# Expert rows gathered in quarter rows through one buffer and turned by VectorE, with the activation transposes amid the next block's gate products

## The chip, the cores and the metric

The kernel runs on one core of one Trainium2 chip. A core has TensorE (matrix products and transposes, written to eight PSUM banks), VectorE, ScalarE, GpSimd (POOL in the profile) and SyncE (SP), which here issues DMAs. Sixteen DMA engines move data for all of them; SP's DMAs stand in one queue of the profile (q1), POOL's in another (q0). The metric is the device time of one execution in microseconds, the median of several runs.

## The reference, cut to what matters

One inference step of a hybrid decoder layer for 1024 prompt tokens and 64 sample tokens (1088 rows of 1024 floats, all float32). Three residual sublayers stand one after the other: attention and a convolution, cross attention to a memory, and a mixture of experts. The change concerns the last:

```python
x = x + hier_moe(rmsnorm(x, norm_ffn_g), w_rg, b_rg, w_re, b_re, w_gate, w_up, w_down)

def hier_moe(h, w_rg, b_rg, w_re, b_re, w_gate, w_up, w_down):
    lg = t @ w_rg + b_rg                       # 4 groups, the best is taken
    le = (t @ w_re + b_re).reshape(-1, 4, 8)   # its 8 experts, the best 2 are taken
    ...
    act = jax.nn.silu(t @ w_gate[e]) * (t @ w_up[e]) * comb[:, e]
    y = sum over the chosen e of act @ w_down[e]
```

There are 32 experts, each with gate and up weights of 1024x256 and down weights of 256x1024, 1 MB apiece. A token goes to two experts.

## The kernel before

**Stages.** Up to about 600 us of the span come the mixer and the sample group's part; then the prompt's cross attention tile by tile (nine tiles of tokens, tile 0 is the 64 sample tokens), with the router of each tile in it. In that stage VectorE writes Z3, the tile's rows after the norm and without the gain, which are stored to a scratch tensor in DRAM, z3 (`z_scratch` in the profile). Z3 is written with its columns permuted (`by_row`), so that column k * 128 + p holds feature 8p + k, the order in which the experts' weights are loaded. TensorE turns Z3 for the router, and VectorE multiplies by the gain vector (`V_FFN` in `cvec`) as it takes the result out of PSUM (line 2318). A sort on VectorE and TensorE then makes the lists: `TABLE`, `PERM` and `PSEL` are multiplied on TensorE (`place`) into the indices of the tokens of each block.

**Blocks.** The experts are computed in 24 blocks (`NB`) of 128 rows, each divided into four parts of 32 rows (`PART`); a part belongs to one expert, and a block has one, two or more experts (`COLUMNS`, in the order `BLOCKS`). `tiles_of(n)` gives each part its weight slot. Seven slots hold the weights of seven experts; the other 25 experts are loaded by SP during the blocks, gate and up as soon as the gate products of the last block that uses a slot are done (`gu_done`), down as soon as its down products are (`dn_done`). A row list has unfilled places; their index lies out of bounds and the DMA drops the row. Rows beyond the lists' room would go through a loop at the end, which has no instruction in this trace.

**A block's path.** POOL gathers its 128 rows of 4 KB from z3 into `ZG` (one buffer, an indirect DMA, line 760). TensorE turns them, eight transposes of 128x128 into banks 0 and 1 (`turn_rows`, line 1388, semaphore `zt4_done`). VectorE takes them out with the gain into `HG[n % 2]` (`take_rows`, line 2430, `hg_ready`). TensorE computes gate and up (`gate_up`, line 1401, 64 instructions, four parts side by side), ScalarE the silu (1793), VectorE the product with up and the token's gate (`activate`, line 2434, `ab_ready`). TensorE turns that with two transposes (line 1431, `at_done`), ScalarE copies them out (1795, `at_ready`), TensorE computes down (`down`, line 1408, 32 instructions), ScalarE and VectorE take the halves out (1800, 2450), and POOL adds the rows to the outputs with two indirect DMAs (766 for the prompt's, 768 for the sample's; rows of the other output are dropped).

**Order.** It is written out by hand. TensorE's step n is: gate and up of block n + 1, activation transposes of block n, row transposes of block n + 2, down of block n. VectorE's step n: activation of n, rows of n + 2, second half of n's result. POOL's loop issues the gather of block n + 1 when block n has been turned, then the adds of block n - 3. SP's loop issues weights as slots come free. Every semaphore is waited for by the engine's own program, in that order.

Of the kernel before, what the change touches and what calls it, by code (L numbers as in the profile page):

```python
# [38 lines left out]
def rank_of(g, j):  # L39
# [16 lines left out]
assert BLOCKS[0] == 0 and [c[2:4] for c in COLUMNS[0]] == [(0, 2), (0, 2)]  # L56
QUARTER = [[k for k, b in enumerate(COLUMNS) if len(b) == 2 and b[1][2:4] == (q, 1)] for q in range(5)]
NSEL = len(FIRST) + len(SECOND)
CONSTS = [("ident", 128), ("mean", 128), ("dist", 256), ("dist_s", 772), ("tri", 128), ("sel", NSEL + 2), ("caps", NE), ("ones", 128),
          ("iota", POS), ("tri33", 33), ("tok", NT), ("thr", 8), ("o16", OVER)]  # L60
# [8 lines left out]
def shape_constants():  # L69
# [23 lines left out]
    put("iota", np.tile(np.arange(POS)[None, :], (128, 1)))  # L93
    put("tri33", (np.arange(32)[:, None] < np.arange(33)[None, :]) * 1.0)
# [44 lines left out]
def build(nc, i, o):  # L139
# [7 lines left out]
    with ctx:  # L147
# [26 lines left out]
        rid_i = sb("rid_i", NE, i32)  # L174
        cap_e = sb("cap_e", 1)
# [88 lines left out]
        tri, sel, caps, ones, iota, tri33, tok, thr, o16 = (rc(n) for n in ("tri", "sel", "caps", "ones", "iota", "tri33", "tok", "thr", "o16"))  # L264
# [39 lines left out]
        HG = [view(W, ROUT + 2048 + 1024 * r, DC, 128) for r in range(2)]  # L304
        YB = [view(W, ROUT + 4096 + 1024 * r, D) for r in range(2)] + [view(W, ROUT + 1024, D)]
        EB = [view(W, ROUT + 6144 + 256 * r, FE) for r in range(2)]
# [51 lines left out]
        for name, (first, count) in {  # L358
# [30 lines left out]
            "over_t": ("zt4_done", 2 * NB),  # L389
            "over_h": ("hg_ready", 2 * NB),  # L390
# [89 lines left out]

        def spread_pt(mt, b):
# [22 lines left out]
        def _(sp):  # L504
# [18 lines left out]
            sp.dma_start(cvec[:, V_FFN:V_FFN + DC], i["norm_ffn_g"][0].rearrange("(p c) -> p c", c=DC)).then_inc(M["small_in"], 16)  # L523
# [9 lines left out]
            sp.dma_start(wr[:, :, 0:NG], i["w_router_group"][0].rearrange("(p c) n -> p c n", c=DC)).then_inc(M["wr_in"], 16)  # L533
            sp.dma_start(wr[:, :, NG:36], i["w_router_expert"][0].rearrange("(p c) n -> p c n", c=DC)).then_inc(M["wr_in"], 16)
# [88 lines left out]
            for it in range(NT + 2):  # L623
# [13 lines left out]
                if s2 == 0:  # L637
# [12 lines left out]
                    load_mo(4, DC)  # L650
                if s2 == NT - 1:
# [55 lines left out]
        def _(pool):  # L707
# [55 lines left out]

            def add_rows(at_p, at_s, buf, landed):
# [1738 lines left out]
```

## Time and profile before

| | us |
|---|---|
| median of 3 runs | 1276.28 (1275.07 to 1276.29) |
| the profiled execution | 1268.7 |
| its span, first to last instruction | 1266.9 |
| TensorE busy | 1168.5 (92%) |
| VectorE busy | 675.2 (53%) |
| ScalarE busy | 323.1 (26%) |
| POOL busy | 146.8 (12%) |
| mean granted TensorE clock | 0.968 |

Times in the rows are microseconds from the start of the span unless marked ns. "idle before" is what the engine stood still ahead of an instruction, with what ended it. PE is TensorE, PEld its loading of the stationary operand, which runs beside the products; DVE is VectorE, ACT ScalarE. A transpose is a matrix product with the identity and stands in the profile as MATMUL. A float32 product stands as two instructions, a transpose as one. The DMA share is the mean busy share of the sixteen DMA engines; since the packets' times overlap a little it can pass 1.

### The profile page before, as it was taken

The numbers are of one execution on the slowest core, as the hardware profiler recorded it, in microseconds if no ns is written. First come the engines' busy times: TensorE is split into PE (matmuls) and PEld (weight loads), VectorE is DVE, ScalarE is ACT, GpSimd is POOL, SyncE is SP. The second block draws the span as 40 slices with busy tenths as digits, with TensorE's granted clock in tenths as the row PEclk, the third lists the DMA queues.
The fourth block names the chain that finished last, engine by engine and source line by source line (L and its number), as shares of the span: only waits on it lengthen the run. The fifth ranks groups of instructions, "written<-read, shape, count | busy, mean of one in ns | idle before, by whom it ended". The sixth has DMA issues, their size and how long they took to land.

```text
span 1266.9 us, 17480 instructions
## 1 busy us (share of the span) xinstructions
PE 1168.5 (92%) x6415; PEld 594.5 (47%) x6415; DVE 675.2 (53%) x2085; ACT 323.1 (26%) x934; POOL 146.8 (12%) x159
## 2 busy tenths in 40 slices
PE   6988879999999999998999999999787999999995
PEld 3434536545555555553555565556442333333331
DVE  1118689999999999831345454545554222222220
ACT  1124434443453456421111111111110101110110
POOL 0000000000000000300000000000001223333332
PEclk9997899999999999999999999999897999999997
DMA  8871000030000002357110011000587998999992
GB/s 317 306 252 46 1 1 26 17 150 34 1 34 34 1 26 114 151 205 312 33 51 23 28 50 50 34 1 34 207 355 311 397 336 319 364 378 385 387 332 53
DMA packets 48914, 194.89 MB, mean 154 GB/s; under 512 B 12240, under 2 KB 15094, under 8 KB 36515
## 3 DMA queue, kind: packets, MB, share of 16 engines
q1 hardware_dynamic: 37883, 173.79, 35.3%
q0 software_dynamic: 10368, 17.87, 5.8%
q10 hardware_dynamic: 576, 2.10, 0.4%
q8 instruction: 52, 0.85, 0.3%
q14 instruction: 35, 0.29, 0.1%
HBM read 172.60 MB, written 42.36 MB: 170 GB/s over the span
## 4 chain that ended last, share of the span: by engine, by line
PE 50%; DVE 4%; DMA 2%; issue 1%; ACT 0%; POOL 0%; SPq 0%; POOLq 0%; DVEq 0%
PE bank L1401 13%; PE bank L843 9%; PE bank L1347 9%; PE bank L1408 7%; PE bank L1325 3%; PE bank L1285 2%; PE bank L1388 2%; PE bank L1126 1%; DMA W<-in_w_mo 1%; DMA W<-in_cache_mem_k 1%; PE bank L1204 1%; DVE G L1848 1%; PE bank L1431 1%; DMA W<-z_scratch,idx_i 1%; PE bank L849 1%
## 5 line engine op out<-in xcount | busy, mean ns | idle before, releaser
L843 PE MATMUL bank<-W,G 128*128 128x512 f32 (+1 forms) x768 | 314.6, 565 | 3.8 <-DVE G L1848 3.0
L1904 DVE SCALAR_TENSOR_TENSOR W<-W,dwT 128x128 f32<-128x128 f32 (+1 forms) x1048 | 271.8, 335 | 0.0
L843 PEld LDWEIGHTS bank<-W,G 128*128 128x128 f32 x768 | 145.4, 192 | 151.0 <-issue 147.6
L1401 PE MATMUL bank<-W 128*32 128x512 f32 x1152 | 155.8, 595 | 1.0 <-DVE W L2430 0.9
L1347 PE MATMUL bank<-W 128*128 128x512 f32 x256 | 115.2, 599 | 0.2 <-DVE W L2309 0.2
L715 POOL TENSOR_SCALAR st<-st 128x1 f32<-128x1 f32 (+3 forms) x40 | 13.7, 343 | 874.7 <-DVE st L2005 434.1
L1126 PE MATMUL bank<-W 128*128 128x512 f32 x256 | 111.8, 594 | 0.0
L2430 DVE TENSOR_TENSOR W<-bank,cvec 128x512 f32<-128x512 f32 x48 | 31.0, 686 | 145.7 <-PE bank L1388 145.7
L1401 PEld LDWEIGHTS bank<-W 128*32 128x32 f32 x1152 | 43.7, 110 | 82.5 <-issue 80.9
L1408 PE MATMUL bank<-W 128*32 128x512 f32 x576 | 81.7, 602 | 0.5 <-ACT W L1795 0.5
L1126 PEld LDWEIGHTS bank<-W 128*128 128x128 f32 x256 | 47.9, 190 | 57.4 <-issue 56.9
L1347 PEld LDWEIGHTS bank<-W 128*128 128x128 f32 x256 | 46.7, 190 | 51.6 <-issue 51.5
L1401 PE MATMUL bank<-G,W 128*32 128x512 f32 x384 | 63.4, 592 | 1.5 <-issue 1.5
L2450 DVE COPY W<-bank 128x512 f32<-128x512 f32 x24 | 16.6, 691 | 81.9 <-PE bank L1408 81.9
L1795 ACT ACTIVATE W<-bank 128x256 f32<-128x256 f32 x24 | 9.2, 383 | 188.2 <-PE bank L1431 188.2
L1841 DVE TENSOR_SCALAR G<-G,st 128x1024 f32<-128x1024 f32 (+1 forms) x20 | 15.0, 752 | 62.7 <-POOL st L719 53.7
L760 POOL DMA_INDIRECT W<-z_scratch,idx_i x24 | 25.5, 1064 | 182.7 <-PE bank L1388 165.8
L1602 ACT ACTIVATE W<-W,st 128x256 f32<-128x256 f32 (+2 forms) x68 | 32.5, 479 | 39.2 <-DVE st L1969 39.2
L766 POOL DMA_INDIRECT out_y_p<-W,idx_i x24 | 37.8, 1576 | 28.0 <-issue 10.7
L768 POOL DMA_INDIRECT out_y_s<-W,samp_i x24 | 37.3, 1554 | 7.3 <-issue 7.3
L1408 PEld LDWEIGHTS bank<-W 128*32 128x32 f32 x576 | 20.2, 110 | 33.9 <-issue 33.2
L1325 PE MATMUL bank<-W,G 128*128 128x128 f32 x256 | 31.8, 284 | 4.2 <-DVE W L2303 4.2
(324 smaller groups left out, 1467.3 us busy)
## 6 DMA issues: line engine op xcount, KB each, us to landing
W<-in_w_exp_gate SPq DMA_DIRECT2D x23, 1024.0 KB
W<-in_w_exp_up SPq DMA_DIRECT2D x23, 1024.0 KB
W<-in_w_exp_down SPq DMA_DIRECT2D x23, 1024.0 KB
G<-in_w_exp_gate SPq DMA_DIRECT2D x9, 1024.0 KB
G<-in_w_exp_up SPq DMA_DIRECT2D x9, 1024.0 KB
G<-in_w_exp_down SPq DMA_DIRECT2D x9, 1024.0 KB
W<-in_cache_mem_k SPq DMA_DIRECT2D x8, 1024.0 KB, 5.0
W<-in_cache_mem_v SPq DMA_DIRECT2D x8, 1024.0 KB, 7.8
```

What stands on the lines that cost most here:

```text
L760: pool.indirect_dma_start(out=buf, out_offset=None, in_=z3_d, in_offset=bass.IndirectOffsetOnAxis(ap=col, axis=0), bounds_check=NTOK - 1, ...
L766: pool.indirect_dma_start(out=yp_flat, out_offset=bass.IndirectOffsetOnAxis(ap=at_p, axis=0), in_=buf, in_offset=None, bounds_check=SEQ - ...
L768: pool.indirect_dma_start(out=ys_flat, out_offset=bass.IndirectOffsetOnAxis(ap=at_s, axis=0), in_=buf, in_offset=None, bounds_check=NS - 1 ...
L843: mm = pe.matmul(bank[0:rows, at:at + hi - lo], HT[:, c, 0:rows], w[:, c, lo:hi], start=(c == 0), stop=(c == DC - 1))
L1126: mm = pe.matmul(B[half][0:n3, :], lhs, w_out[:, c, 512 * half:512 * half + 512], start=(c == 0), stop=(c == 7))
L1325: mm = pe.matmul(B[6 + c // 4][:, (c % 4) * 128:(c % 4) * 128 + 128], MV[:, mt, c * 128:(c + 1) * 128], PT2[:, mt, c // 2, :], start=(mt = ...
L1347: mm = pe.matmul(B[2 + half][0:n2, :], OT2[:, c, 0:n2], w_mo[:, c, 512 * half:512 * half + 512], start=(c == 0), stop=(c == DC - 1))
L1401: mm = pe.matmul(B[2 + par][lo:hi, :], HG[par][:, c, lo:hi], WGU[u][:, :, c, :], start=(c == 0), stop=(c == DC - 1), skip_group_check=True)
L1408: mm = pe.matmul(B[6 + half][lo:hi, :], AT[par][:, c, lo:hi], WD[u][:, c, 512 * half:512 * half + 512], start=(c == 0), stop=(c == 1), ski ...
L1602: act.activation(sh, sh, ACT.Exp, bias=st[:, 50 + h:51 + h], scale=SCALE, accum_out=st[:, 58 + h:59 + h]).then_inc(M["s_exp"], 2 if s2 == ...
L1904: dve.scalar_tensor_tensor(y, src, w, y, ALU.mult, ALU.add).then_inc(M["conv_tap"], 1)
L2430: dve.tensor_tensor(buf[:, 4 * half:4 * half + 4, :], B[half][:, :].rearrange("p (c t) -> p c t", c=4), gain(V_FFN + 4 * half, 4), ALU.mul ...
```

## The change

- **Rows in quarters.** From block 2 (`TURNED`) on, a block's rows come by four indirect DMAs instead of one. Quarter q is 256 columns of `ZG`. On partition 32 s + r it holds segment s (256 floats, 1 KB) of the row r of part q, so each DMA gathers 128 pieces of 1 KB; the indices are 4 * token + s. They are made by 28 small products on TensorE (`place_segments`) and one instruction on VectorE (`seg_i`).
- **Turned by VectorE.** VectorE waits until the four have landed and turns each quarter with one transpose instruction in blocks of 32x32 (`turn_segments`), straight into `HG`, whose layout becomes four parts of 8 x 32. `turn_rows` on TensorE remains for blocks 0 and 1, with a strided read.
- **One buffer.** `ZG` stays the only buffer. The gather of block n + 3 is issued when VectorE has turned block n + 2 (`hg_ready`), and POOL's adds of block n - 1 follow it.
- **Activation transposes.** For blocks 4 to 22 they stand after the first half of the next block's gate products (`within`), otherwise where they were.
- **Gain.** Z3 is written in plain column order and already multiplied by the gain, which comes as a broadcast tile `GB` (loaded by SP behind the w_mo loads, into room that the sample group's scores have left). The router's and the blocks' PSUM reads become plain copies. The router's weights are laid out to match.

```diff
+        def quarters_of(n):
+            return [(q0 + k) * NE + rank_of(g, j) for g, j, q0, count in COLUMNS[BLOCKS[n]] for k in range(count)]
...
+        def rows_landed(n):
+            return 16 * n + 16 if n < TURNED else 16 * TURNED + 64 * (n + 1 - TURNED)
...
+        def rows_turned(n):
+            return 2 * n + 2 if n < TURNED else n + 1 + TURNED
...
+                    sp.wait_ge(M["mkb_used"], DEC_B)
+                    sp.dma_start(GB, i["norm_ffn_g"].to_broadcast([128, D])).then_inc(M["gb_in"], 16)
...
+                if u == 4:
+                    sp.wait_ge(M["z3_ready"], AFTER["z3_ready"] + NT)
                 load_down(sp, expert_id(NEED[u]), u)
...
+            def gather_quarters(n):
+                for q, col in enumerate(quarters_of(n)):
+                    pool.indirect_dma_start(out=ZG[:, 256 * q:256 * q + 256], out_offset=None, in_=z3_segments,
+                                            in_offset=bass.IndirectOffsetOnAxis(ap=seg_i[:, col:col + 1], axis=0),
+                                            bounds_check=4 * NTOK - 1, oob_is_err=False).then_inc(zg_in, 16)
...
-            for n in range(NB + 3):
-                if n + 1 < NB:
-                    pool.wait_ge(M["zt4_done"], 2 * n + 2)
-                    at = BLOCKS[n + 1]
-                    gather(idx_i[:, at:at + 1], zg_in, ZG)
-                if n == 3:
+            gather(idx_i[:, BLOCKS[1]:BLOCKS[1] + 1], zg_in, ZG)
+            pool.wait_ge(M["zt4_done"], 2 * TURNED)
+            pool.wait_ge(M["route_ready"], 3)
+            gather_quarters(TURNED)
+            for n in range(NB + 1):
+                if n + 3 < NB:
+                    pool.wait_ge(M["hg_ready"], rows_turned(n + 2))
+                    gather_quarters(n + 3)
+                if n == 1:
...
-                if n >= 3:
-                    add_block(n - 3)
+                if n >= 1:
+                    add_block(n - 1)
...
+            def place_segments():
+                for q in range(QMAX):
+                    for s in range(4):
+                        mm = pe.matmul(B[7][PART * s:PART * s + PART, NE * q:NE * q + NE], TABLE[0:2 * NE, PART * q:PART * q + PART], PERM[0:2 * NE, :], start=True, stop=True, skip_group_check=True)
+                mm.then_inc(M["r_cols"], 1)
...
+                    if c == DC // 2 and within >= 0:
+                        turn_activation(within)
                     for lo, hi, u in tiles:
-                        mm = pe.matmul(B[2 + par][lo:hi, :], HG[par][:, c, lo:hi], WGU[u][:, :, c, :], start=(c == 0), stop=(c == DC - 1), skip_group_check=True)
+                        mm = pe.matmul(B[2 + par][lo:hi, :], HG[par][:, lo // PART, c, :], WGU[u][:, :, c, :], start=(c == 0), stop=(c == DC - 1), skip_group_check=True)
...
-                    gate_up(tiles_of(n + 1), 1 - p).then_inc(M["gu_done"], 1)
-                pe.wait_ge(M["ab_ready"], n + 1)
...
-                if n + 2 < NB:
-
-                    for mm in turn_rows(n + 3):
-                        mm.then_inc(M["zt4_done"], 1)
+                    gate_up(tiles_of(n + 1), 1 - p, 0, n if n > 3 else -1).then_inc(M["gu_done"], 1)
+                if n <= 3 or n + 1 == NB:
+                    turn_activation(n)
...
-                    dve.tensor_scalar(by_row(Z3[0:n3, :], DC), XB(s3)[0:n3, :].rearrange("p (f c) -> p f c", c=DC), st[0:n3, 41:42], None, ALU.mult).then_inc(M["z3_ready"], 1)
+                    if s3 == 0:
+                        dve.wait_ge(M["gb_in"], AFTER["gb_in"] + 16)
+                    dve.scalar_tensor_tensor(Z3[0:n3, :], XB(s3)[0:n3, :], st[0:n3, 41:42], GB[0:n3, :], ALU.mult, ALU.mult).then_inc(M["z3_ready"], 1)
...
-                        dve.tensor_tensor(H3[:, 4 * half:4 * half + 4, 0:n3], src, gain(V_FFN + 4 * half, 4, n3), ALU.mult).then_inc(M["h3_ready"], 1)
+                        dve.tensor_copy(H3[:, 4 * half:4 * half + 4, 0:n3], src).then_inc(M["h3_ready"], 1)
...
+            def turn_segments(n):
+                dve.wait_ge(zg_in, rows_landed(n))
+                for q in range(4):
+                    a = dve.transpose(HG[n % 2][:, q], ZG[:, 256 * q:256 * q + 256].rearrange("p (f c) -> p c f", c=DC))
+                a.then_inc(M["hg_ready"], 1)
...
                 if n + 2 < NB:
-                    take_rows(None, HG[p], M["zt4_done"], n * 2 + 5, M["hg_ready"])
+                    turn_segments(n + 2)
```

## Rows read from the trace of the kernel before

**Rows 1.** The page's 40 equal slices of the span, TensorE and DMA, in tenths.

```profile
PE   6988879999999999998999999999787999999995
...
DMA  8871000030000002357110011000587998999992
```

**Rows 2.** The critical chain, 1112 to 1142: start, length, engine and line.

```profile
1124.44 0.87 PE bank L1388 x8
...
1136.12 0.87 PE bank L1388 x8
```

**Rows 3.** The timeline of one block and of the last: start, length, engine, line.

```profile
1117.02 7.05 PE L1401 MATMUL bank<-W 128*32 128x512 f32 x64
...
1124.28 1.04 PE L1388 MATMUL bank<-cst,W 128*128 128x128 f32 x8
...
1125.24 3.64 PE L1408 MATMUL bank<-W 128*32 128x512 f32 x32
...
1126.13 1.07 POOL L760 DMA_INDIRECT W<-z_scratch,idx_i  x1 [6.87 <-PE bank L1388]
...
1235.53 0.62 PE L1401 MATMUL bank<-G,W 128*32 128x512 f32 x2 [1.53 <-issue]
```

**Rows 4.** Windows of 20 us: busy time and instructions by engine, clock, DMA share.

```profile
1040.00:1060.00 20.00, 20.00 (x188) 7.22 (x184) 4.88 (x8) 2.51 (x6) 7.54 (x6) 1.00 0.79 266
...
1100.00:1120.00 20.00, 20.00 (x184) 7.14 (x180) 5.16 (x8) 2.51 (x6) 8.40 (x6) 1.00 1.03 374
```

**Rows 5.** SP's issues: down weights (ns, min/median/max), and the last up weight.

```profile
L475 SPq DMA_DIRECT2D W<-in_w_exp_down x23: 337/338/4907, 904.2 to 1204.1; - x23
...
1199.72 3.60 SPq L471 DMA_DIRECT2D G<-in_w_exp_up  x1
```

**Rows 6.** Two lines of VectorE, ns min/median/max: contiguous 256, and strided 1024.

```profile
L2144 DVE TENSOR_SCALAR W<-W,LG x9: 346/353/354, 671.0 to 953.4; 128x256 f32<-128x256 f32 x8, 64x256 f32<-64x256 f32 x1
...
L2267 DVE TENSOR_SCALAR W<-G,st x9: 1294/1337/1354, 611.3 to 941.2; 128x1024 f32<-128x1024 f32 x8, 64x1024 f32<-64x1024 f32 x1
```

**Rows 7.** The critical chain at the stage's first blocks.

```profile
974.23 0.70 issue
974.94 8.53 DMA W<-z_scratch,idx_i
...
988.17 6.87 PE bank L1401 x64
```

**Rows 8.** POOL's lines, 965 to the end: busy us, mean ns, idle before.

```profile
L768 POOL DMA_INDIRECT out_y_s<-W,samp_i x24 | 37.3, 1554 | 7.3 <-issue 7.3
L760 POOL DMA_INDIRECT W<-z_scratch,idx_i x23 | 24.3, 1055 | 165.8 <-PE bank L1388 165.8
```

**Rows 9.** DMA queues in windows 1080:1220, 1138:1141.5, 1142:1145, 1127:1129: packets, MB, share.

```profile
q1 hardware_dynamic: 6020, 43.85, 75.9%
...
q0 software_dynamic: 137, 0.03, 6.8%
...
q1 hardware_dynamic: 108, 0.79, 62.5%
q0 software_dynamic: 108, 0.44, 35.9%
...
q1 hardware_dynamic: 106, 0.78, 92.4%
q0 software_dynamic: 99, 0.03, 8.8%
```

**Rows 10.** The timeline at the start of the stage.

```profile
958.17 1.27 POOL L760 DMA_INDIRECT W<-z_scratch,idx_i  x1 [16.96 <-DVE idx_i L2222]
...
959.18 0.27 PE L1376 MATMUL bank<-W 128*32 128x1 f32 x2 [2.34 <-DVE W L2152]
...
963.35 1.94 PE L1388 MATMUL bank<-cst,W 128*128 128x128 f32 x8 [0.43 <-DMA W<-z_scratch,idx_i]
```

**Rows 11.** Windows around a fall of the granted clock (third number from the right).

```profile
595.00:598.20 3.20, 0.66 (x4) 0.42 (x4) 1.48 (x3) 1.87 (x4) 0.00 (x0) 1.00 0.97 389
598.20:601.60 3.40, 2.74 (x8) 0.89 (x10) 1.02 (x2) 0.53 (x2) 1.95 (x4) 0.50 0.03 6
```

More of the change, by code:

```diff
@@ L56 @@
 assert BLOCKS[0] == 0 and [c[2:4] for c in COLUMNS[0]] == [(0, 2), (0, 2)]
+QMAX = max(max(c) for c in CAPS)
+TURNED = 2
 QUARTER = [[k for k, b in enumerate(COLUMNS) if len(b) == 2 and b[1][2:4] == (q, 1)] for q in range(5)]
@@ L263, in rc @@
             return RC[:, lo:lo + CAT[name][1] - CAT[name][0]]
[L264 removed]
+        tri, sel, caps, ones, iota, seg, tri33, tok, thr, o16 = (rc(n) for n in ("tri", "sel", "caps", "ones", "iota", "seg", "tri33", "tok", "thr", "o16"))
         LG3 = view(LG, 0, NT, 36)
@@ L303, in build @@
         ZG = view(W, ROUT, D)
-        HG = [view(W, ROUT + 2048 + 1024 * r, DC, 128) for r in range(2)]
+        HG = [view(W, ROUT + 2048 + 1024 * r, 4, DC, 32) for r in range(2)]
         YB = [view(W, ROUT + 4096 + 1024 * r, D) for r in range(2)] + [view(W, ROUT + 1024, D)]
+        GB = view(W, 12288, D)
         EB = [view(W, ROUT + 6144 + 256 * r, FE) for r in range(2)]
@@ L1382, in turn_rows @@
             def turn_rows(count):
-                pe.wait_ge(zg_in, 16 * count)
+                pe.wait_ge(zg_in, count)
+                rows = ZG.rearrange("p (f c) -> p c f", c=DC)
                 for half in range(2):
@@ L1387, in turn_rows @@
                         k = 4 * half + c
-                        mm = pe.transpose(B[half][:, c * 128:(c + 1) * 128], ZG[:, k * 128:(k + 1) * 128], ident)
+                        mm = pe.transpose(B[half][:, c * 128:(c + 1) * 128], rows[:, k, :], ident)
                     yield mm
@@ L1394, in tiles_of, with turn_activation, gate_up @@
                 return [(PART * k, PART * k + PART, u) for k, u in enumerate(slots)]
-            def gate_up(tiles, par, upper=0):
+            def turn_activation(n):
+                p = n % 2
+                pe.wait_ge(M["ab_ready"], n + 1)
+                if n == 3:
+                    pe.wait_ge(M["r_taken"], AFTER["r_taken"] + 1)
+                for c in range(2):
+                    mm = pe.transpose(B[4 + p][:, c * 128:(c + 1) * 128], AB[p][:, c * 128:(c + 1) * 128], ident)
+                mm.then_inc(M["at_done"], 1)
+            def gate_up(tiles, par, upper=0, within=-1):
                 for c in range(DC):
@@ L1449, in _ @@
             pe.wait_ge(M["route_ready"], 2)
-            for mm in turn_rows(1):
+            for mm in turn_rows(16):
                 mm.then_inc(M["zt4_done"], 1)
@@ L1454, in _ @@
             gate_up(tiles_of(0), 0, 2).then_inc(M["gu_done"], 1)
-            for mm in turn_rows(2):
+            for mm in turn_rows(32):
                 mm.then_inc(M["zt4_done"], 1)
@@ L1469, in _ @@
                 with pe.Fori(1, OVER + 1) as n:
-                    for mm in turn_rows(n + NB):
+                    for mm in turn_rows(n * 16 + ROWS0):
                         mm.then_inc(M["over_t"], 1)
@@ L1473, in _ @@
                     pe.wait_ge(wgu_in[0], n * 32 + 32 * LOADS[0])
-                    gate_up([(0, 128, 0)], 0).then_inc(M["over_gu"], 1)
+                    gate_up([(PART * k, PART * k + PART, 0) for k in range(4)], 0).then_inc(M["over_gu"], 1)
                     pe.wait_ge(M["ab_ready"], n + NB)
@@ L2424, in over_list, with take_rows @@
                 dve.tensor_copy(gate_s[:, NR:NSLOT], got[:, 1, :]).then_inc(M["over_listed"], 1)
-            def take_rows(banks, buf, done, count, ready):
+            def take_rows(buf, done, count, ready):
                 for half in range(2):
                     dve.wait_ge(done, count + half)
-                    dve.tensor_tensor(buf[:, 4 * half:4 * half + 4, :], B[half][:, :].rearrange("p (c t) -> p c t", c=4), gain(V_FFN + 4 * half, 4), ALU.mult).then_inc(ready, 1)
+                    dve.tensor_copy(buf[:, :, 4 * half:4 * half + 4, :], B[half][:, :].rearrange("p (c q t) -> p q c t", c=4, q=4)).then_inc(ready, 1)
+            def turn_segments(n):
[3 more added lines that the diff above has]
+                a.then_inc(M["hg_ready"], 1)
             def activate(p, e, a, gate):
```

42 lines of the change are left out of this document (23 added, 19 removed).

## The prediction

> **What bounds the kernel now.** I read the page's slices first. In the eight before the last, the expert stage, TensorE stands at 9 in all and the DMA engines at 9 in seven [rows 1]. Two resources are full at once, so the stage has to be read for both.
>
> Then the critical chain: from block 2 to block 22 it is TensorE over and over, gate and up products (L1401), two transposes of the activation (L1431), eight of the next rows (L1388), down products (L1408), with a period of 11.68 us (1124.44 to 1136.12) and no wait [rows 2]. The timeline of one block splits it [rows 3]: gate and up products start at 1117.02, the row transposes at 1124.28, the down products at 1125.24, the next block's gate products 11.68 after the first. The row transposes take 1125.24 - 1124.28 = 0.96 us.
>
> The windows say how full the DMA engines are: 1.03 at 1100 to 1120 and much the same in the windows around it, with one real hole, 0.79 at 1040 to 1060 [rows 4]. The SP queue says it again: a down weight takes 0.338 us to issue in the median but up to 4.9, and the last up weight 3.6, at 1199.72: its queue is full [rows 5]. At the end TensorE stands still for 1.53 us (1234.0 to 1235.53) before the last gate and up products [rows 3], and the row names no engine that it waited for; the weights of the last block were queued on SP only at 1199.72 [rows 5]. So the stage is bound by TensorE by a hair, and TensorE's lead over the weights is used up by its end.
>
> **TensorE, removed.** 22 blocks lose 0.96 us each, 21.1 us. The two activation transposes go into the middle of the next gate products from block 4 on; their time stays, and the array is drained and filled once more there: the products' last start lies at most 0.5 us before the transposes now, I take +0.1. ScalarE's copy then lies under the second half of the gate products, where before it lay under the row transposes: costs nothing. TensorE alone would need 10.8 us a block.
>
> **VectorE.** It loses two PSUM reads a block and gets four transposes of 128x256 each. The trace has none. Nearest rows: 128x256 from SBUF 0.353 us, and a 128x1024 with a strided side 1.33 us, or 0.33 for each 256 [rows 6]. Below: four at 0.3, 1.2 us; above: four at twice the row, 2.8. I take the row itself, 4 x 0.35 = 1.4 us. VectorE is busy 5 of 20 us in the stage [rows 4], so as work it is nothing; but it now stands in a loop.
>
> **The loop through the one buffer.** Before, a gather was issued when TensorE had turned the rows ahead of it, at 1126.13, and had 9.8 us until the transposes 11.68 after 1124.28 wanted it [rows 3]. Now the gather of n+3 is issued when VectorE has turned n+2, and VectorE turns n+3 when all four quarters have landed. These steps follow each other and set a period of their own:
>
> - VectorE done to POOL's first issue: 0.75 (the chain has 0.70 before the issue at 974.94 [rows 7]).
> - Four issues instead of one, each 1.06 [rows 8] with the 0.30 between that the adds show (7.3 us / 24): 1.38 apart, the last starts 4.1 after the first. With two adds of 1.55 and 0.30 POOL needs 9.2 us a block; it fits.
> - Issue to first row: 4.0 us. The gather issued 11.68 us after that of 1126.13, at 1137.81 [rows 3], has moved nothing by 1141.5: POOL's queue shows 137 packets but 0.03 MB in 1138 to 1141.5 (those are the dropped rows of the adds); then in 1142 to 1145 it moves 0.44 MB [rows 9].
> - How the two queues share the engines: 108 packets against 108 in 1142 to 1145, when rows of 4 KB meet weight packets of 8 KB; 99 against 106 in 1127 to 1129, when POOL's packets are nearly all under 512 B [rows 9]. One for one, whatever their size. A weight packet of 8 KB costs 0.759 x 16 x 140 us / 43.85 MB x 8192 B = 0.318 us of one engine [rows 9]. So a gather of 128 rows is 8 packets an engine and waits for 8 weight packets. Check: 4.0 + 8 x (0.16 + 0.318) = 7.8, measured 8.53 to landing [rows 7]: 0.7 for completion.
> - In quarters the gather is 512 packets, 32 an engine. Their own time is small, 1.0 us together (a 4 KB row at half of the 8 KB packet, 0.16; a quarter of that for a quarter row; less for dropped rows). The weight packets between them are not: between 0 and 32 x 0.318 = 10.2 us.
>
> How many meet? 25 experts are loaded in the stage, 24 packets an engine each, over 22 blocks: 27 a block. POOL's queue has 32 + 16 (adds) = 48 a block to pair with them. If the 27 spread evenly over the 48, the gather meets 18: 5.7 us. The period is then 0.75 + 4.0 + (1.0 + 5.7) + 0.7 + 0.1 + 1.4 = **13.65 us**. Once no weights load (the last three intervals) the fourth issue sets it: 0.75 + 4.1 + 4.0 + 0.3 + 0.7 + 0.1 + 1.4 = **11.35**. Ends: none meet, 11.35; all 27, 16.5.
>
> DMA time is no tighter bound. Before, with the holes of [rows 4], it filled nearly all of 11.68; the smaller packets add some 0.2: 11.9 us a block, under 13.65.
>
> The Trainium skill ("DMA: Bandwidth & Descriptors", Queues, rings and completion order) says an engine alternates between queues by packets of several descriptors, typically 9 to 17. By that four or more quarter rows would go for one weight packet, and this loop would not bind (the second rival). The rows on single 4 KB and 8 B pieces speak against it here.
>
> **Start of the stage.** 28 small products (56 instructions) for the quarter lists come on TensorE ahead of that line (L1376). It stands idle for 2.34 us before 959.18 [rows 10]. Four run side by side, as the expert products do (64 in 7.05 us, 16 groups of 0.43 of 512 columns [rows 3]); with 32 columns 0.18 a group is ample: 14 x 0.18 = 2.5 us, so little shows, +0.5. If each of the 56 took 0.12 as one of the eight transposes does (0.96 / 8), 6.7 us, of which 3.5 would show.
>
> **Edits at nothing.** The gain vector's multiplication moves from the router's PSUM reads, which stay as copies of the same size, into the write of Z3 (1.33 us [rows 6], same size, no stride now); nine times a tenth either way. Its 0.5 MB broadcast is queued on SP behind the w_mo loads, for which the output products before the first Z3 wait anyway; were it late, the first tile would wait its 0.5 MB, 1 to 2 us. SP's two new waits, for the score products and for the last Z3, ask for what its next DMA comes after in any case: the sample group's memory values are freed later than its scores are made, and Z3 of the last tile is stored ahead of slot 4's down weights. POOL's adds keep their place, one block's behind one gather.
>
> **Sum, against the profiled execution** (span 1266.9, time 1268.7; the median of the three runs, 1276.28, is 7.6 above it). The chain has block 2's gate products at 988.2, block 23's start at 1235.5 [rows 3, 7]. After: the quarters of block 2 are issued at 974.94 with four weight loads just queued, so all 32 meet: 974.94 + 4.0 + 11.2 + 0.7 + 0.1 + 1.4 = 992.3. Then 18 intervals of 13.65 and 3 of 11.35: 992.3 + 245.7 + 34.1 = 1272.1, +0.5 = 1272.6. That is 37.1 later than 1235.5; the tail of 31.4 us stays. 1276.3 + 37.1 = **1313 us**.
>
> **Rivals.**
> - *Packets of four quarter rows.* Four pieces of 1 KB go at one turn, as the one row of 4 KB did. The gather meets 8 weight packets, 2.5 us, and the period falls to 11.35, under the DMA engines' 11.9. Block 2 starts at 986.1, 2 us sooner, since TensorE no longer waits for rows ahead of the down products; 986.1 + 18 x 11.9 + 3 x 11.35 = 1234.4: **1276**, no change, for the removed transposes only run into the weights. For it: the full DMA share and SP's queue. Against: one for one in both windows.
> - *Faster* (the other side). The same, and the first row comes 2 us after the issue, not 4: the very first gather, of 4 KB rows, took only from 958.17 to TensorE's start on it at 963.35 [rows 10]. The loop is 9.4, TensorE's 10.8 decides until the weights do, and the holes in DMA time (4 us in that of [rows 4]) are filled: **1271**. It decides from the point where the loop is under 11.7. 21 us are not to be had, the weights forbid it.
> - *The clock.* TensorE now stands still for 13.65 - 10.8 = 2.9 us a block. The granted clock was 0.50, the 1.2 GHz level, for 598.2 to 601.6, right after 3.2 us in which TensorE was busy for 0.66 [rows 11]. One such dip of 3.4 us costs 1.7 us: 12.5, still under 13.65. If it stayed at 1.2 GHz (groups of twice 0.43, 24 of them, 21 us a block) it would be 1276 + 21 x 7.7 + 31 = **1470**.
>
> **How the numbers follow.** Main case 0.64; packets of four 0.22; faster 0.10; clock 0.04. The range takes the main case with a turn of 2.8 us (21 x 1.4 = 29 more, 1343) above, and nearly all of "no change" below, 1273; left out are the faster case, the clock, and gathers that meet all 27. 0.2%, 2.5 us, is about what a measurement of this kernel tells from no change. Faster: 0.10 and 0.04 of the second case; same: 0.09 of it; slower: the rest.
>
> **What would show it.** Right: gaps on TensorE before the gate products that end with VectorE's transposes, those waiting for z_scratch DMAs; blocks of uneven length, about 11.4 without and 14 to 18 with weight loads; DMA share under 1; SP's issues back at 0.34 us. Wrong: a period under 12 us, quarters landing under 9 us after the first issue while weights load, or packet counts of POOL's queue well above the weights' in such a window.

## The result: slower, by a third to a little over half of what was forecast

| | kernel before | changed kernel |
|---|---|---|
| runs of this comparison, us | 1275.67 median (1271.91 to 1276.29) | 1288.80 median (1286.47 to 1290.92) |
| ratio | | 1.0118, 95% interval 1.0096 to 1.014 |
| profiled execution, time / span, us | 1268.70 / 1266.9 | 1289.27 / 1287.5 |
| mean granted clock | 0.968 | 0.964 |

The forecast was 1313 us, 37.1 more than before; 13.1 were measured. A second comparison of the same two kernels (below) gave 1.0172, interval 1.0148 to 1.0197, which does not meet the first one. So one comparison is uncertain by more than its interval says, and the change costs 13 to 21 us. The two profiled executions lie 20.6 us apart.

The slices of the changed kernel, TensorE and the DMA engines:

```profile
span 1287.5 us, 17419 instructions
...
PE   6989879999999999997999999999759898988795
...
DMA  8871000220100004285011001000978979999963
```

In the expert stage TensorE now shows eights among the nines, and the DMA engines are about as full as before [rows 1]. Who holds up whom is in the chain, from the end of one block's turn to the end of the next (start, length, what):

```profile
1127.65 0.60 DVE W L2490
...
1129.06 0.37 POOL W L793
...
1131.78 1.00 POOL W L793
1132.78 0.30 issue
1133.09 6.00 DMA W<-z_scratch,WR
...
1139.11 0.30 DVE W L2490
...
1139.67 1.64 DVE W L2490 x3
```

TensorE is gone from the chain that it filled before [rows 2]. VectorE ends its turn (the four transposes of a block) at 1128.26; POOL's first gather begins at 1129.06; the fourth is under way from 1133.09; the rows are there at 1139.09; four transposes end at 1141.31. That is the loop of the forecast, 13.05 us here. The groups of the page (busy, mean ns, idle before), the waits of TensorE from 990 to 1260, and the last two blocks on its timeline:

```profile
L2490 DVE STREAM_TRANSPOSE W<-W 128x256 f32<-128x256 f32 x88 | 48.7, 613 | 198.4 <-DMA W<-z_scratch,WR 198.4
...
L793 POOL DMA_INDIRECT W<-z_scratch,WR x88 | 90.0, 1023 | 120.0 <-DVE W L2490 90.4
```

```profile
PE bank L1460 <- DVE W L2490: 31.5, 17, 3.4
```

```profile
1235.89 3.64 PE L1460 MATMUL bank<-W 128*32 128x512 f32 x32 [2.47 <-DVE W L2490]
...
1246.72 3.62 PE L1460 MATMUL bank<-W 128*32 128x512 f32 x32
...
1257.53 0.60 PE L1460 MATMUL bank<-G,W 128*32 128x512 f32 x2
```

Block 23 starts its gate products at 1257.5 where it was 1235.5 [rows 3]. The last two intervals are 10.8 us, once no weights load: that is the period which the prediction gave TensorE alone, where it had 11.35 for the last three. Before that it waited for VectorE 17 times, 31.5 us in all.

The windows (busy us and instructions by engine, clock, DMA share, GB/s) say that the DMA engines did not get idler, although a block takes longer [rows 4]:

```profile
1100.00:1120.00 20.00, 17.17 (x140) 4.61 (x132) 5.26 (x10) 1.26 (x3) 11.20 (x10) 0.91 1.01 373
1140.00:1160.00 20.00, 18.22 (x148) 5.13 (x152) 5.85 (x11) 1.64 (x4) 11.14 (x10) 0.91 1.03 380
```

The weights run on at the engines' rate and get ahead of TensorE: the gate and up weights of block 23 landed at 1236.6, 20.9 us before their use, where before it was 1235.4 and 0.1 us.

**How the quarter rows travel.** The DMA queues from 1000 to 1220, the changed kernel and then the kernel before (packets, MB, share; the sizes in the first line are cumulative):

```profile
DMA packets 16838, 77.62 MB, mean 353 GB/s; under 512 B 5818, under 2 KB 5838, under 8 KB 8913
...
q0 software_dynamic: 7925, 12.58, 24.2%
...
W<-z_scratch,WR POOLq DMA_INDIRECT x68
```

```profile
DMA packets 17143, 80.01 MB, mean 364 GB/s; under 512 B 5660, under 2 KB 5660, under 8 KB 9133
...
q0 software_dynamic: 8132, 14.26, 25.9%
```

68 gathers of quarter rows, and only 5838 - 5818 = 20 packets of 512 B to 2 KB. Between 2 and 8 KB there are 8913 - 5838 = 3075, or 181 for each of 17 blocks; before 3473, or 183 for each of 19. These are the rows of the gather and those of the adds together. Of the 3075, 3027 have 4096 B to the byte, all in POOL's queue, and their lengths fall into two heaps: 1467 of about 0.16 us, 86 a block, and the rest of about 0.33. The first are the gathers': when the adds are cut to 16 rows (below), 1489 of them are left, and 308 of the others. Quarter rows alone would be four times 86. Four quarter rows ride in one packet. The Trainium skill ("DMA: Bandwidth & Descriptors", SWDGE vs HWDGE vs iDMA) says this of DMAs issued from GpSimd: a packet is preferably at most 4096 B and at most 64 descriptors, and it is the boundary at which an engine changes queues. By that, four pieces of 1 KB, and one row of 4 KB, both fill a packet, which is what these rows show; the prediction weighed only the page's "9 to 17" and missed this line.

### The profile page after: what moved, and what is told of

It is laid out like the page before. It is cut to its first block, busy times and chain, and to the rows that moved or that the text cites. A ratio compares the mean times of both kernels' runs of the same rounds, so it can differ in the third digit from the quotient of the medians.

```text
span 1287.5 us, 17419 instructions
## 1 busy us (share of the span) xinstructions
PE 1159.2 (90%) x6295; PEld 574.9 (45%) x6295; DVE 694.0 (54%) x2130; ACT 323.0 (25%) x934; POOL 214.9 (17%) x225
## 3 DMA queue, kind: packets, MB, share of 16 engines
q1 hardware_dynamic: 37883, 174.31, 35.1%
## 4 chain that ended last, share of the span: by engine, by line
PE 31%; DMA 11%; DVE 7%; issue 6%; POOL 3%; ACT 0%; POOLq 0%; SPq 0%; DVEq 0%
DMA W<-z_scratch,WR 9%; PE bank L880 9%; PE bank L1384 8%; DVE W L2490 3%; PE bank L1362 3%; POOL W L793 2%; PE bank L1460 2%; PE bank L1322 2%; PE bank L1163 1%; PE bank L1467 1%; DMA W<-in_w_mo 1%; DMA W<-in_cache_mem_k 1%; PE bank L886 1%; PE bank L1241 1%; DVE G L1899 1%
## 5 line engine op out<-in xcount | busy, mean ns | idle before, releaser
L1460 PE MATMUL bank<-W 128*32 128x512 f32 x1152 | 164.9, 617 | 27.0 <-DVE W L2490 25.9
L2490 DVE STREAM_TRANSPOSE W<-W 128x256 f32<-128x256 f32 x88 | 48.7, 613 | 198.4 <-DMA W<-z_scratch,WR 198.4
L793 POOL DMA_INDIRECT W<-z_scratch,WR x88 | 90.0, 1023 | 120.0 <-DVE W L2490 90.4
L1467 PE MATMUL bank<-W 128*32 128x512 f32 x576 | 79.6, 593 | 1.4 <-ACT W L1846 1.4
L1851 ACT ACTIVATE W<-bank 128x512 f32<-128x512 f32 x24 | 14.3, 597 | 105.2 <-PE bank L1467 105.2
## 6 DMA issues: line engine op xcount, KB each, us to landing
G<-in_w_exp_up SPq DMA_DIRECT2D x9, 1024.0 KB, 13.1
```

The costliest lines, as they stand in the source:

```text
L793: pool.indirect_dma_start(out=ZG[:, 256 * q:256 * q + 256], out_offset=None, in_=z3_segments, in_offset=bass.IndirectOffsetOnAxis(ap=seg_i ...
L1460: mm = pe.matmul(B[2 + par][lo:hi, :], HG[par][:, lo // PART, c, :], WGU[u][:, :, c, :], start=(c == 0), stop=(c == DC - 1), skip_group_ch ...
L1467: mm = pe.matmul(B[6 + half][lo:hi, :], AT[par][:, c, lo:hi], WD[u][:, c, 512 * half:512 * half + 512], start=(c == 0), stop=(c == 1), ski ...
L2490: a = dve.transpose(HG[n % 2][:, q], ZG[:, 256 * q:256 * q + 256].rearrange("p (f c) -> p c f", c=DC))
```

## The experiments

The first ratio is that of the result's comparison; the others are to runs of the kernel before on the same chip (medians 1272.27, 1271.20 and 1271.42 us in three sets). Profiled executions start block 0 anywhere from 963.4 to 970.5 us, at mean clocks from 0.959 to 0.970, so traces are compared from block 2 on. The columns are worked out from them: the start of the first gate products of blocks 2 and 23, their distance over 21 (the period), and for gathers issued from 995 to 1220 the mean time from the first issue's start to the last one's end, from there to the last landing, and for the block's transposes.

| kernel | ratio (95%) | block 2 | block 23 | period | issues | landing | turn |
|---|---|---|---|---|---|---|---|
| before | 1 | 988.0 | 1235.5 | 11.79 | | | |
| changed | 1.0118 (1.0096 to 1.014) | 989.4 | 1257.5 | 12.77 | 5.02 | 4.88 | 2.21 |
| changed, again | 1.0172 (1.0148 to 1.0197) | 989.9 | 1258.7 | 12.80 | 5.02 | 4.90 | 2.21 |
| amid alone | 1.0029 (1.0008 to 1.005) | 993.2 | 1244.2 | 11.95 | | | |
| behind the gate products | 1.0227 (1.0196 to 1.0258) | 992.9 | 1268.0 | 13.10 | 5.02 | 5.01 | 2.24 |
| two transposes | 1.0089 (1.0058 to 1.012) | 984.7 | 1245.7 | 12.43 | 5.04 | 5.47 | 1.16 |
| side by side source | one run | 987.9 | 1250.7 | 12.52 | 5.05 | 5.30 | 1.42 |
| half copies | one run | 988.6 | 1254.5 | 12.66 | 5.03 | 5.24 | 1.74 |
| adds of 16 rows | 1.0061 (1.0042 to 1.0081) | 989.7 | 1246.9 | 12.25 | 5.00 | 4.29 | 2.22 |
| one gather | 0.9967 (0.9946 to 0.9987) | 985.5 | 1231.6 | 11.72 | 1.06 | 7.67 | 2.23 |
| eighth of the weights | 0.9843 (0.9823 to 0.9862) | 990.6 | 1219.4 | 10.89 | 5.05 | 2.70 | 2.26 |
| before, eighth of the weights | 0.9969 (0.9953 to 0.9986) | 986.7 | 1232.5 | 11.71 | | | |
| quarter by quarter | 0.9994 (0.9977 to 1.0011) | 987.5 | 1235.6 | 11.82 | | | |
| quarter by quarter, eighth | 0.9834 (0.9813 to 0.9855) | 990.9 | 1219.5 | 10.88 | | | |

**1. Where the activation transposes stand.** In the kernel before, that part alone:

```diff
-                    gate_up(tiles_of(n + 1), 1 - p).then_inc(M["gu_done"], 1)
-                pe.wait_ge(M["ab_ready"], n + 1)
+                    gate_up(tiles_of(n + 1), 1 - p, 0, n if n > 3 else -1).then_inc(M["gu_done"], 1)
+                if n <= 3 or n + 1 == NB:
+                    turn_activation(n)
```

> The kernel before with one part of the change alone: the two activation transposes of a block go amid the next block's gate products; the rows still come whole and are turned by TensorE. Theory (the loop of gather issue, landing and VectorE's turn sets the changed kernel's period, and the placement costs nothing): the period of the gate products stays at 11.7 us and the time within 0.3% of the kernel before, 1272 to 1279 us. Rival (the placement makes TensorE stand amid the products for the activation, 0.5 us or more a block over 20 blocks): 10 us or more slower, 1286 us or above, and the placement alone would be most of the measured +13.

1276.10 us, 0.29% over before, as the theory had it. The chain, this kernel and then the kernel before:

```profile
1124.71 3.43 PE bank L1412 x32
1128.15 0.37 PE bank L1402 x2
1128.52 3.57 PE bank L1412 x32
1132.09 1.02 PE bank L1388 x8
1133.11 3.57 PE bank L1419 x32
```

```profile
1113.63 3.57 PE bank L1408 x32
1117.20 6.87 PE bank L1401 x64
1124.07 0.37 PE bank L1431 x2
```

There is no wait, yet 3.43 + 3.57 are 0.13 more than 6.87, and the row transposes, now right behind products, take 1.02 where they took 0.87 [rows 2]. So it costs 0.28 us a block where TensorE is the bound (0.1 was forecast). From block 2 to 23 that is 3.5 us by the table (251.0 against 247.5), since this kernel has no wait of 1.5 us before its last block [rows 3]. The reverse, in the changed kernel:

```diff
-                    gate_up(tiles_of(n + 1), 1 - p, 0, n if n > 3 else -1).then_inc(M["gu_done"], 1)
+                    gate_up(tiles_of(n + 1), 1 - p).then_inc(M["gu_done"], 1)
-                if n <= 3 or n + 1 == NB:
-                    turn_activation(n)
+                turn_activation(n)
```

> The changed kernel with the activation transposes behind the next block's gate products, as before; the quarter rows stay. Theory (the loop sets the period): the down products come a little later, nothing else moves; 1284 to 1293 us, a period of 12.8 us. Rival (the placement costs): 10 us or more faster than the changed kernel, 1278 us or below.

1299.63 us: neither. Without the row transposes nothing lies between the activation's transposes and the down products, and TensorE waits for ScalarE's copy (1000 to 1220):

```profile
L1467 PE MATMUL bank<-W 128*32 128x512 f32 x400 | 63.2, 628 | 16.1 <-ACT W L1845 16.1
L2489 DVE STREAM_TRANSPOSE W<-W 128x256 f32<-128x256 f32 x68 | 38.1, 616 | 141.3 <-DMA W<-z_scratch,WR 141.3
L1467 PE MATMUL bank<-G,W 128*32 128x512 f32 x144 | 30.5, 712 | 9.7 <-ACT W L1845 9.7
```

25.8 us over 17 blocks (544 instructions, 32 a block), of which the period shows 0.3 a block; the rest lies beside the loop, which the chain still follows. Since this set and the first could differ by chance:

> The changed kernel once more, beside the runs of the kernel before on the chip of this set, to put the kernel with the activation transposes behind the gate products (2.27% over before) against it: 1.0 to 1.4% over before if the placement matters in the changed kernel by 10 us; 1.9% or more if the two are alike and the first sets differed by chance.

1292.71 us, 1.72% over: between the two. By the traces, 0.30 to 0.33 us of period, 6 to 7 us, are the placement's, and 2.27% against 1.72% is 7 us too; the 14 us between 2.27% and 1.18% would be too much. Amid the products is the better place in the changed kernel, and it is not what makes it slow.

**2. The turn.** Two of four transposes a block are left out (half of the rows stay stale):

```diff
-                for q in range(4):
+                for q in range(2):
                     a = dve.transpose(HG[n % 2][:, q], ...
```

> The changed kernel, of whose four VectorE transposes of a block in blocks 2 to 23 only the first two are done, so half of the turned rows is stale. Theory (each transpose of 0.6 us lies in the loop): the period falls by 1.1 to 1.2 us to 11.6, over 21 blocks minus 23 us: 1264 to 1270 us. If the weights' transfers are the bound (a bound of 11.7 to 11.9 us from the bytes): the period falls only to 11.9, and the time to 1270 to 1276. Rival (the turn is hidden behind other work): no change, 1289 us.

1282.13 us, where the theory had 1264 to 1270. The turn fell by 1.05 us, nearly as said; the landing grew from 4.88 to 5.47, and the period fell by 0.34 instead of 1.1. My theory of steps with fixed lengths fell here: the same weights now fall on shorter blocks, and more of them travel beside a gather's rows (11.2 packets an engine, against 9.4 in the changed kernel; how they are counted stands under 3). One landing of this kernel in the chain:

```profile
1123.36 7.95 DMA W<-z_scratch,WR
```

Why is one transpose 0.61 us? Two edits, each run once. In the first edit the values come in another order, in the second half of them aren't turned:

```diff
-dve.transpose(HG[n % 2][:, q], ZG[...].rearrange("p (f c) -> p c f", c=DC))
+dve.transpose(HG[n % 2][:, q], ZG[...].rearrange("p (c f) -> p c f", c=DC))
```

> The changed kernel, whose VectorE transposes read 256 columns that lie side by side, where they step over eight (the values are then in another order). If the step is what makes one of them 0.61 us where 0.35 was forecast: 0.35 to 0.40 us each, and 1.0 us less in the loop's turn. Rival (the transpose itself costs it): 0.6 us each and no change in the loop.

```diff
+                    if q < 2:
                         a = dve.transpose(...)
+                    else:
+                        a = dve.tensor_copy(HG[n % 2][:, q], ZG[...].rearrange("p (f c) -> p c f", c=DC))
```

> The changed kernel, in which the third and fourth VectorE transpose of a block are plain copies of the same shape and the same stepped source (that half is then not turned). If the transpose operation is what costs: copies of 0.35 us beside transposes of 0.61. If the stepped source is: both at 0.6 us.

The groups on VectorE, source side by side, and then with half copies:

```profile
L2490 DVE STREAM_TRANSPOSE W<-W 128x256 f32<-128x256 f32 x69 | 24.6, 413 | 162.6 <-DMA W<-z_scratch,WR 162.6
```

```profile
L2491 DVE STREAM_TRANSPOSE W<-W 128x256 f32<-128x256 f32 x36 | 20.9, 619 | 171.1 <-DMA W<-z_scratch,WR 171.1
...
L2493 DVE COPY W<-W 128x256 f32<-128x256 f32 x36 | 11.8, 369 | 0.0
```

A stepped copy costs 0.37, a transpose of a close-packed source 0.41, a stepped transpose 0.61: it takes both. The step explains 0.20 of the 0.26 us by which it is over the 0.35 that I took. Times were 1284.14 and 1287.99 us; the loop again gave part back (landings of 5.30 and 5.24).

**3. What the landing is made of.** The adds of a block cover 16 of 128 rows:

```diff
-...ap=at_p, axis=0), in_=buf, in_offset=None,
+...ap=at_p[0:16], axis=0), in_=buf[0:16], in_offset=None,
```

(and the same for `at_s`).

> The changed kernel, whose two adds of a block's result cover only 16 of its 128 rows. Theory (a gather's packets go behind the adds of the block before in POOL's queue, and alternate with the weights' packets): the landing after the fourth issue falls from 4.9 to 3.5 us or less, the period from 12.9 to 11.6 or less, 1262 to 1275 us. Rival (only the gather's own packets and the weights' set the landing): the landing stays at 4.5 us or more and the time within 6 us of the changed kernel.

1278.35 us and a period of 12.25; the landing is 4.29, so 0.6 of its 4.9 us go with the adds. That is less than I said, and more than the rival. It makes up the 11 us by which this kernel is earlier than the changed one from block 2 to 23; the last block's shorter adds give another 4.

The packets of the two traces say how. The gathers' are the ones of 0.16 us. In the changed kernel, in the mean of the 17 blocks, the first of them starts 4.23 us after the first issue; the last ends 4.35 us later, and meanwhile an engine moves 9.4 weight packets of 8 KB; the landing follows after 1.33 more. With the short adds the three are 4.14, 3.97 and 1.20, with 7.8 weight packets. So the adds hardly hold up the first row, and my theory that the gather stands behind them is not what the trace shows: most of the 0.6 us is in the rows themselves, which travel faster. How much of that is the engine time which the adds no longer take (92 packets of 0.33 us a block, an estimate of 1.9 us of each engine) no run tells.

The weights: the 25 loads in the stage move 16 of 128 partitions (the products use stale weights):

```diff
-            eng.dma_start(WGU[u][:, 0], expert_rows("w_exp_gate", e, DC)).then_inc(wgu_in[u], 16)
+            eng.dma_start(WGU[u][0:rows, 0], expert_rows("w_exp_gate", e, DC)[0:rows]).then_inc(wgu_in[u], 16)
```

> The changed kernel, whose 25 loads of expert weights within the stage move only 16 of 128 partitions (the products use stale weights). Theory (the loop of reaction 0.8, four issues 5.0, landing 4.9 and turn 2.2 us sets the period, and the weights' packets make up more than half of the landing): the landing falls to 1.1 to 1.8 us, as in the last blocks of the changed kernel, the loop to 9.6 us, and TensorE's 10.8 us becomes the period: 42 to 46 us faster than the changed kernel, 1241 to 1247 us. Rival (the issues and turns set it, whatever the weights do): the period stays above 12 us.

> The kernel before, with the same loads of 16 of 128 partitions. Theory (TensorE's 11.68 us sets its period and the weights only the last 1.5 us gap): 0 to 4 us faster, a period of 11.68. Rival (the transfers' rate sets the period of the kernel before too): a period below 11.3 us and 10 us or more faster.

1251.21 and 1267.73 us. The changed kernel gains 35 us or more (35 by its first ratio, 42 by its second; 42 to 46 were expected), the kernel before 3.5, as its theory had it. The chain of the changed kernel, 1000 to 1220, is TensorE's again:

```profile
by line: PE bank L1460 64.0%; PE bank L1467 32.3%; PE bank L1449 3.4%; ACT W L1846 0.2%; PE bank L1490 0.2%; PE bank L1491 0.1%; issue 0.0%
```

Its landing fell to 2.70, not to 1.1 to 1.8 (loads of 16 partitions still meet the gathers here and there), so its loop of 10.8 is just level with TensorE. Part of the fall is in the wait for the first row. In the changed kernel's own trace the last two gathers, with no weights left, have their first row packet 1.8 and 2.1 us after the first issue, where the 17 of the table needed 4.2 in the mean.

**4. The four issues.** One gather of whole rows fills the buffer (rows of other experts then stand in three quarters of it):

```diff
-                for q, col in enumerate(quarters_of(n)):
-                    pool.indirect_dma_start(out=ZG[:, 256 * q:256 * q + 256], ...
+                gather(idx_i[:, BLOCKS[n]:BLOCKS[n] + 1], zg_in, ZG)
```

> The changed kernel, in which one gather of whole rows fills the buffer instead of four of quarter rows (the rows' quarters are then those of other experts); four VectorE transposes, one buffer and all waits stay. Theory (the issues lie in series in the loop): three issues of 1.33 us, 4.0 us, leave the loop; the landing takes part of that back, since the gather then comes earlier behind the adds of the block before, as two transposes less gave back 0.6 of 1.1 us; the period falls to 11.0 to 11.8 us and the time to the floor of the last weights, 1266 to 1274 us. Rival (bytes and turns set it, the issues are hidden): within 5 us of the changed kernel.

1266.26 us and a period of 11.72, as the theory had it, though far more came back in the landing than the 0.6 it leant on. Its chain:

```profile
1126.42 1.12 DVE W L2487 x2
1127.54 0.58 DVE W L2508
...
1128.36 8.98 DMA W<-z_scratch,idx_i
```

From the start of the first issue to the landing it is 1.06 + 7.67 = 8.73 us, with four issues 9.90. Three issues of 1.33 us cost 1.17 together, because they lie beside the wait for the first row: it comes 4.16 us after the first issue with one gather and 4.23 with four, whose last issue starts at 4.0.

**5. A loop that overlaps, and the floor.** Each quarter is gathered as soon as VectorE has turned that quarter of the block before, and turned when it has landed (the semaphores for it are taken over from earlier stages, an edit not shown):

```diff
                 for q, col in enumerate(quarters_of(n)):
+                    if n > TURNED:
+                        pool.wait_ge(q_turned, Q0 + 4 * (n - 1 - TURNED) + q + 1)
                     pool.indirect_dma_start(out=ZG[:, 256 * q:256 * q + 256], ...
-                                            ...).then_inc(zg_in, 16)
+                                            ...).then_inc(q_in[q], 16)
...
                 for q in range(4):
+                    dve.wait_ge(q_in[q], 16 * (n + 1 if q == 0 else n - TURNED + 1))
-                    a = dve.transpose(HG[n % 2][:, q], ...
+                    dve.transpose(HG[n % 2][:, q], ...).then_inc(q_turned, 1)
```

> The changed kernel, but each of the four gathers of a block is issued as soon as VectorE has turned the same quarter of the block before, and each quarter is turned when its own gather has landed (a semaphore for each quarter). Theory (the loop in series, 0.8 + 4.0 + 6.0 + 2.2 us, sets the period): the issues of later quarters go beside the turns, so the loop shortens by the 1.8 us of three transposes or more, and the period falls to what the transfers allow, 11.5 to 11.9 us, or TensorE's 10.8: 1262 to 1276 us. Rival (the transfers' rate sets the period, with 3 times the gather's packets): the period stays at 12.5 or more and the time above 1283 us.

1271.14 us against 1272.27: as fast as before, no faster. The loop is shorter than the 11.68 of before (the 18 intervals from block 3 to 21 have a mean of 11.46), though not down to TensorE's 10.8, and 47.0% of the chain from 1000 to 1220 is still the gathers' landings. But block 23 starts at 1235.6, to 0.1 us where the kernel before starts it [rows 3]. The timeline, then windows with the granted clock in the column before the DMA share:

```profile
1221.91 3.64 PE L1467 MATMUL bank<-W 128*32 128x512 f32 x32
...
1235.63 1.07 PE L1467 MATMUL bank<-G,W 128*32 128x512 f32 x2 [6.64 <-issue]
...
1236.45 1.09 PE L1467 MATMUL bank<-G,W 128*32 128x512 f32 x2
```

```profile
1230.00:1235.00 5.00, 0.00 (x0) 0.00 (x0) 0.38 (x1) 0.00 (x0) 1.76 (x2) 0.89 0.50 161
1235.00:1240.00 5.00, 4.37 (x24) 1.25 (x28) 0.00 (x0) 0.00 (x0) 1.35 (x1) 0.50 0.77 164
1240.00:1245.00 5.00, 5.00 (x46) 1.40 (x42) 0.00 (x0) 0.38 (x1) 0.00 (x0) 0.92 0.09 21
```

TensorE stood still for 6.64 us, until the last gate and up weights were there at 1235.6. The clock fell to the 1.2 GHz level within that gap, and TensorE then worked for about 5 us at it. Is it the weights that both wait for?

> The kernel with gathers issued quarter by quarter, with the same loads of 16 of 128 partitions. In the run with full weights its last gate products waited 18.3 us after those before, where TensorE needs 10.8, and they began as early as in the kernel before. Theory (there the arrival of the last weights is a floor common to all versions): with an eighth of the bytes the period is TensorE's 10.8 us throughout and the time falls to 1240 to 1247 us. Rival (the quarter-by-quarter loop is itself the bound at 11.5 us): 1260 us or more.

With the short loads: 1250.71 us, a period of 10.88 and no gap before block 23. (The sum behind my 1240 to 1247 was careless: 989.4 + 21 x 10.88 + 31.4 and the 1.8 around the span make 1251.) With full weights, the gate and up weights of block 23 are in place 270.1 us after the start of block 0 in the kernel before, 269.6 in the changed one, 269.3 in this, 267.2 with two transposes and 267.1 with one gather, whatever TensorE does meanwhile (block 23 itself starts between 267.4 and 290.6). With adds of 16 rows it is 251.3: the floor goes with the bytes. The windows from block 0 on to 1232, of before and of this kernel, say why: in the mean the engines are hardly ever free.

```profile
970.00:1232.00 262.00, 260.10 (x2360) 91.55 (x2356) 58.61 (x97) 27.11 (x65) 89.06 (x64) 1.00 0.97 360
```

```profile
970.00:1232.00 262.00, 253.33 (x2208) 80.29 (x2200) 83.77 (x143) 28.02 (x67) 157.08 (x130) 1.00 0.99 363
```

So none of the versions measured that move all these bytes got the 21 us of removed transposes; the best, with one gather, which computes with wrong rows, is 0.33% faster than before, 4 to 5 us. TensorE's lead is spent on waiting for the last weights. Whether the floor itself could come earlier was not tried. In the last microseconds before it the sixteen engines are not all busy (0.50 from 1230 to 1235 above), and the shares of the last gate and up loads land one after the other from 246.7 to 269.3 us after the start of block 0, so most shares are there well before the last one.

## Why the forecast had the sign and not the size

- **TensorE's period of 10.8 us**: right, in the last intervals and with few weights. **The loop through the one buffer** as the new bound: right, and its place is the chain's.
- **The step that failed: "in quarters the gather is 512 packets, 32 an engine", and so 18 weight packets between them, 5.7 us.** The quarters ride four to a packet; the gather kept its size in packets, 86 a block of 4096 B, 5.4 an engine. Beside its rows the trace counts 9.4 weight packets an engine instead of 18, 3.0 us at the 0.318 of the prediction. From the first issue to the landing the forecast had 4.0 + 6.7 + 0.7 = 11.4 us, the trace 4.23 + 4.35 + 1.33 = 9.9. That is 1.5 us a block too much, and it stands in the term of 6.7; the two others were a little too small.
- **The turn** was mis-sized the other way: 1.4 us, measured 2.21, since a stepped transpose takes 0.61. The bound of 2.8 held it. With 0.82 for 0.75 of reaction the loop is 0.82 + 5.02 + 4.88 + 0.02 + 2.21 = 12.95, not 13.65. So the forecast of the period was only 0.7 off because two errors went against each other; that part is luck.
- **Once no weights load**: 11.35 forecast, 10.8 measured, and that is TensorE's. The loop itself was still shorter. The prediction kept its 4.0 us from issue to first row, which it had read where weights load; without them it was 1.8 and 2.1, and in the last two blocks the landing came 1.2 and 1.8 us after the last issue. With the reaction, the issues and the turn that is 9.2 and 9.9 us.
- **The sum.** Block 2 came at 989.4, not 992.3: 2.9 us; the 21 intervals took 268.1, not 279.8 (the first 18 took 233.0 for 245.7, the last three 35.1 for 34.1): 11.7; the start of the stage cost 0.5 less; the tail was 1.4 shorter. Together 16.5, and 37.1 - 16.5 = 20.6 is what lies between the two profiled executions. The other 7.5 us to the median's 13.1 are the profiled execution of before, 7 us under its own median; the second comparison, 21.3 us, suggests that they belong to the noise.
- **Start of the stage.** The 56 products (start of the group and length, on TensorE's timeline):

```profile
958.38 0.97 PE L1414 MATMUL bank<-W,G 64*32 64x32 f32 x56
```

  0.97 us for 2.5 forecast, inside a wait: nothing. The edits put at nothing: block 0 starts at 967.0, within the spread of the other executions, so no run contradicts it.
- **Amid the products**: +0.1 forecast, 0.28 measured where TensorE is the bound; in the changed kernel it is a gain of 0.3 over the other place.
- **The rivals.** "Packets of four quarter rows" had the mechanism (0.22 was too low), and not the time: its 11.35 us held a turn of 1.4 and 4.1 + 4.0 + 0.3 + 0.7 = 9.1 us from the first issue to the landing, where 2.21 and 9.90 were measured, and its 1276 us come only when the loop overlaps, as in the run quarter by quarter. "Faster" did not come; its first row 2 us after the issue is what the runs show without weights, and not with them. The clock: the dips that this rival priced came, three of them, 3.4 us each at the 1.2 GHz level, from 1115.3, 1142.6 and 1169.9 (the first two lie in the windows with 0.91 above), where the kernel before has none. TensorE's products don't appear in the chain from 1000 to 1220, so they cost nothing there: its waits took them up. In the run quarter by quarter the level held from 1233.9 to 1240.8.
- **"DMA share under 1"** as a sign was wrong: weights and gathers draw each other out. Take 1.05 us from the loop and the landing gives 0.6 back; take three issues and it gives 2.8 back. With an eighth of the weights it fell from 4.9 to 2.7. Why the first row takes 4.2 us with weights in the queues and 1.8 without stays open. The sign for being wrong, quarters landing under 9 us after the first issue, did not show in the mean (9.9) although the packet term was wrong: it was set too close to the rival's 9.1 to tell the two apart.

## What to carry to other kernels

When several small gathers replace one, count packets by size in a window before pricing them: pieces may share a packet. Price a loop through one buffer with the DMA engines full as they are, and expect part of each saving to come back as a longer landing. And if two resources are full at once, a saving on one is worth only its lead until the other's last arrival; here that was 4 to 5 us at most, so little but the loop's cost showed. A wait read while the queues are full, as the 4 us to the first row, is not a constant either.

## What the runs showed of the hardware, unexpected

- Indirect gathers of 1 KB pieces move in packets of 4096 B (20 of 16838 packets lie between 512 B and 2 KB). Such a packet of a gather takes 0.16 us, one of 4096 B of an add 0.33.
- From the first issue of a gather to its first row: 4.2 us with weight loads in the other queue, whether the rows come by one gather or four; 1.8 to 2.1 us without.
- VectorE's 128x256 f32 transpose: 0.61 us from a source stepping over eight, 0.41 from one side by side; the stepped copy 0.37.
- 56 products of 64 by 32 with 32 columns took 0.97 us, 17 ns each with four side by side.
- Two comparisons of the same pair of kernels on two occasions gave 1.0118 and 1.0172, with intervals that do not meet.
